# Which heads share a logits group in the sparse attention of a two-layer streaming encoder

## The reference, cut to what matters

```python
score = einsum('bqhs,bqh->bqs', relu(dots), wi)           # indexer, 8 heads of 64
top_val, top_idx = lax.top_k(score, k_top)                # 128 keys, 144 for the sample
qg = q.reshape(B, QB, N_KV_HEADS, KV_GROUP, HEAD_DIM)     # 8 heads = 2 KV heads x 4, each 64 wide
logits = einsum('bqngd,bqknd->bqngk', qg, k_sel) * HEAD_DIM ** -0.5
p = softmax(where(valid, logits, -inf))
o = einsum('bqngk,bqknd->bqngd', p, v_sel)
mix = concat([o, y_conv]); x = x + gt_a * (mix @ w_out)
```

## Time and profile before

| | |
|---|---|
| median of 3 runs | 1521.48 us (1521.14 to 1523.52) |
| the profiled execution | 1521.48 us |
| its span, first to last instruction | 1519.7 us |
| outside the span | 1.8 us |
| mean granted TensorE clock | 0.879 of 2.4 GHz |
| attention groups, layer 0 | about 333 to 436 us |
| attention groups, layer 1 | about 1078 to 1181 us |

### The profile page before, as it was taken

One profiled execution on the slowest core, in us unless ns is written; L12 is line 12 of the kernel. 1 busy time (PEld: TensorE's weight loads), 2 busy tenths in 40 slices (PEclk: granted clock), 3 DMA queues, 4 the chain that ended last, 5 costly groups with the idle time before them and its releaser, 6 DMA issues. The chain is left out here.

```text
span 1519.7 us, 14104 instructions
## 1 busy us (share of the span) xinstructions
PE 1218.0 (80%) x5211; PEld 726.5 (48%) x5211; DVE 752.3 (50%) x1541; ACT 336.3 (22%) x756; POOL 480.3 (32%) x292
## 2 busy tenths in 40 slices
PE   4699888945899878999708997896377995999980
PEld 0354525332445466777505544362245454777760
DVE  1109999787625521111151299998783353211114
ACT  2110231233431111111131003302535111111112
POOL 0005999443620120000020079995156011000002
PEclk9899999965999879999958998598758997999995
DMA  9961385340860579999581003011003016699975
GB/s 359 350 231 56 121 287 188 112 174 1 281 240 28 181 256 331 369 364 365 189 304 29 8 28 118 0 63 55 9 15 63 0 58 229 219 366 362 367 260 187
DMA packets 139300, 274.45 MB, mean 181 GB/s; under 512 B 16308, under 2 KB 98588, under 8 KB 132830
## 3 DMA queue, kind: packets, MB, share of 16 engines
q1 hardware_dynamic: 110272, 199.31, 38.2%
q10 hardware_dynamic: 22398, 50.63, 9.9%
q0 software_dynamic: 6560, 23.60, 4.3%
HBM read 237.89 MB, written 52.40 MB: 191 GB/s over the span
## 5 line engine op out<-in xcount | busy, mean ns | idle before, releaser
L409 PE MATMUL ps<-W,arena 128*128 128x256 f32 (+1 forms) x1280 | 348.4, 428 | 10.0 <-DMA W<-in_w_gate 4.6
L409 PEld LDWEIGHTS ps<-W,arena 128*128 128x128 f32 x1280 | 242.6, 193 | 85.6 <-issue 55.3
L419 PE MATMUL ps<-C,arena 128*128 128x128 f32 (+3 forms) x851 | 129.4, 301 | 113.1 <-DVE arena L1311 25.4
L409 PE MATMUL ps<-W,hT 128*128 128x512 f32 (+5 forms) x640 | 193.5, 463 | 1.6 <-DVE gt L1164 1.6
L419 PEld LDWEIGHTS ps<-C,arena 128*128 128x128 f32 (+3 forms) x851 | 107.8, 161 | 147.7 <-issue 52.6
L1238 DVE SCALAR_TENSOR_TENSOR arena<-arena,taps 128x606 f32<-128x606 f32 x180 | 158.9, 955 | 0.2
L1608 POOL TENSOR_TENSOR arena<-arena 128x512 f32<-128x512 f32 x8 | 89.6, 11202 | 208.0 <-ACT arena L898 208.0
L1666 POOL DMA_INDIRECT arena<-y_d,sid x20 | 20.2, 1009 | 404.4 <-DMA y_d<-arena 200.9
L409 PEld LDWEIGHTS ps<-W,hT 128*128 128x128 f32 (+1 forms) x640 | 103.5, 183 | 91.8 <-issue 82.4
L648 PE MATMUL ps<-W,hT 128*128 128x512 f32 (+1 forms) x320 | 143.3, 601 | 1.0 <-issue 1.0
L409 PE MATMUL ps<-hT,W 128*128 128x64 f32 (+1 forms) x512 | 140.5, 437 | 3.6 <-ACT hT L869 3.6
(11 more groups left out here) (217 smaller groups left out, 1167.5 us busy)
## 6 DMA issues: line engine op xcount, KB each, us to landing
W<-in_w_ada SPq DMA_DIRECT2D x48, 1024.0 KB, 6.5
W<-in_w_gate SPq DMA_DIRECT2D x32, 1024.0 KB, 10.6
W<-in_w_up SPq DMA_DIRECT2D x32, 1024.0 KB, 12.9
W<-in_w_down SPq DMA_DIRECT2D x32, 1024.0 KB, 7.8
arena<-x_d SPq DMA_DIRECT2D x33, 512.0 KB, 11.2
y_d<-arena ACTq DMA_DIRECT2D x33, 512.0 KB, 7.2
W<-in_w_in SPq DMA_DIRECT2D x16, 1024.0 KB, 14.6
W<-in_w_out SPq DMA_DIRECT2D x8, 1024.0 KB, 6.5
```

Source lines behind the costliest of these rows:

```text
L409: ins = T.matmul(out, l, r, start=n == 0, stop=n == len(pairs) - 1, skip_group_check=True)
L419: count(T.transpose(o, i, ident[0:m, 0:m]), done if n == len(outs_ins) - 1 else None)
```

## The change

Which four heads make a group is changed. Before, group (t, g) takes heads from both KV heads: jobs j = 0 to 3 are i = 2g, 2g, 2g + 1, 2g + 1, in the lower, upper, lower, upper half of the rows. After, group (t, g) takes the four heads of KV head g: all four jobs are in the same half, lower for g = 0 and upper for g = 1. The bank of a job and the waits are the same by job number.

PV follows: a group has one KV head, so one value matrix serves two heads in one product with twice the columns. There are half as many PV matmuls, each over 2m columns instead of m (m is 128, or 64 in the sample tile). `outputs` writes to `hT` chunks 2g, 2g + 1 instead of g, g + 2.

```diff
                 def logits(n):
-                    t, half = GROUPS[n]
+                    t, g = GROUPS[n]
                     a, b = keys_of(t)
-                    for j in range(4):
-                        job, i = 4 * n + j, 2 * half + j // 2
-                        hp = slice(64 * (j % 2), 64 * (j % 2) + 64)
+                    hp = slice(64 * g, 64 * g + 64)
+                    for i in range(4):
+                        job = 4 * n + i
                         if job >= 3:
                             pe.wait_ge(L["ttr"], job - 1 if 2 <= n <= 4 else job - 2)
                         q = qT[hp, i, tokens(t)]
...
-                    for q in range(2):
-                        for c, kn in chunks_of(t):
-                            v = (...)[:, 64 * q:64 * q + 64]
-                            heads = pT[0:kn, c, 0:4 * m].rearrange("p (a g t) -> p a g t", a=2, g=2)
-                            for a in range(2):
-                                ins = T.matmul(ps[6 + n % 2][64 * a:64 * a + 64, q * m:(q + 1) * m], v, heads[:, a, q, :],
-                                               start=c == 0, stop=c == last, skip_group_check=True)
+                    for c, kn in chunks_of(t):
+                        v = (...)[:, g * 64:g * 64 + 64]
+                        heads = pT[0:kn, c, 0:4 * m].rearrange("p (j a t) -> p j a t", j=2, a=2)
+                        for a in range(2):
+                            ins = T.matmul(ps[6 + n % 2][64 * a:64 * a + 64, 0:2 * m], v, heads[:, :, a, :],
+                                           start=c == 0, stop=c == last, skip_group_check=True)
...
-                    S.copy(hT[:, g:g + 3:2, t * P:t * P + m],
+                    S.copy(hT[:, 2 * g:2 * g + 2, t * P:t * P + m],
```

More of the change, by code:

```diff
@@ L608, in _ @@
                     pe.wait_ge(L["pta"], PT0[n] + len(chunks_of(t)))
-                    for q in range(2):
-                        for c, kn in chunks_of(t):
-                            v = (vrow[0:kn, c, :] if t < 4 else cv[:, c, :] if c < 4 else vrow[0:kn, 4, :])[:, 64 * q:64 * q + 64]
-                            heads = pT[0:kn, c, 0:4 * m].rearrange("p (a g t) -> p a g t", a=2, g=2)
-                            for a in range(2):
-                                ins = T.matmul(ps[6 + n % 2][64 * a:64 * a + 64, q * m:(q + 1) * m], v, heads[:, a, q, :],
-                                               start=c == 0, stop=c == last, skip_group_check=True)
+                    for c, kn in chunks_of(t):
+                        v = (vrow[0:kn, c, :] if t < 4 else cv[:, c, :] if c < 4 else vrow[0:kn, 4, :])[:, g * 64:g * 64 + 64]
+                        heads = pT[0:kn, c, 0:4 * m].rearrange("p (j a t) -> p j a t", j=2, a=2)
+                        for a in range(2):
+                            ins = T.matmul(ps[6 + n % 2][64 * a:64 * a + 64, 0:2 * m], v, heads[:, :, a, :],
+                                           start=c == 0, stop=c == last, skip_group_check=True)
                     ins.then_inc(L["pv"], 1)
```

## The result

The changed kernel takes 1539.6 us in the median (1535.7 to 1542.5) beside 1522.0 for the kernel before. The ratio is 1.0115 with a 95% interval of 1.0097 to 1.0133, so it is about 17.6 us slower. The forecast was 1530 with a range up to 1537: the sign was right, the size half of what came. The profiled execution took 1542.4 us (span 1540.4).

The account below looks back on a forecast made before the run. Attention was taken as a relay of engines, with logits groups on the path. 1521.5 us plus 8.7 for serial logits (4.3 in layer 0, 4.4 in layer 1) minus 0.1 for PV gave 1530.1, range 1525 to 1537.

Parts of the forecast that it names:

- the mechanism and its fixed price: Logits: jobs in opposite row halves overlapped, now run one after the other; 4.3 us in layer 0, 4.4 in layer 1.
- the forecast with clocks as before: Main case: TensorE's granted clock stays as it was, 1527 to 1533 us; 58 in 100.
- the 0 for groups 5 and 6 of layer 0: Logits of these two groups in layer 0: the serial order was claimed to cost 0 in each.
- the clock goes the wrong way: Rival, layer 1: 1.2 GHz lasts longer, group 2 +2.5 us or group 7 +3; 1532.5 or both 1535.5; 25 in 100.
- TensorE finishes three jobs before VectorE arrives: Group 5 of layer 0: the fourth job is alone anyway, so serial order costs 0.
- queues on GpSimd: Group 6 of layer 0: +0.2 at 2.4 GHz, but its normalising product waits behind group 5's, so 0.
- group 4 of layer 1: Logits: the same stall on VectorE as in layer 0, hidden since group 5 starts from GpSimd; 0.
- group 6 of layer 1: Logits over 384 keys at 1.2 GHz: serial 5.48 us against 4.06, +1.4.
- exposed loads: Rival: weight loads into the working row half can't be hidden, 12.8 us more, 1543; 3 in 100.
- nothing behind takes the delay in: After attention: no DMA wait absorbs the delay, so the rest shifts; output projections start at about 441 and 1190 us.
- Its own price: PV: paid by column, so half the matmuls at twice the columns gives -0.1 us; bounds -4.6 to +0.9.

Follow-up runs that it names:

- e0: The kernel before, unchanged, run again for a second profile and the scatter of its times; ratio 0.9999 (0.998 to 1.0017).
- e5: The changed kernel with PV cut back into narrow matmuls of one head each, a repeat on another chip; ratio 1.0090 (1.0063 to 1.0116).
- e2: The changed kernel with PV cut back into narrow matmuls of one head each; ratio 1.0056 (1.0033 to 1.0078).
- e9: The changed kernel with seven unused matmuls per layer in groups 3 and 4, where TensorE waits; ratio 1.0071 (1.0056 to 1.0086).
- e4: The changed kernel, unchanged, run again for a second profile; ratio 1.0117 (1.0093 to 1.0142).
- The twins: The changed kernel, each logits job of groups 2 to 9 followed by an unused equal product in the other row half; ratios 1.0019 and 1.0015.
- e6: The kernel before with a fourth PSUM bank for the logits of groups 4 to 9 of layer 1; ratio 0.9994 (0.9977 to 1.0011).
- e3: The changed kernel with an unused equal product in the other row half after each logits job of groups 2 to 9; ratio 1.0019 (1.0000 to 1.0038).
- e10: The changed kernel with the unused products in the other row half, a repeat; ratio 1.0015 (0.9999 to 1.0032).
- e7: The kernel before with seven unused matmuls per layer in groups 3 and 4, where TensorE waits; 1518.5 us, ratio 0.9971 (0.9957 to 0.9984).

## Why the prediction was wrong

**Right: the mechanism and its fixed price.** The halves overlapped and now follow each other; what the forecast worked out from passes came true to a few tenths wherever the clock was the same. That is group 2, 3 and 4 of layer 0, group 3 and 5 of layer 1. TensorE's time of group 6 at 1.2 GHz (5.49 against 5.48) and of group 7 at 2.4 (2.84 against 2.82) did too. At the clock that these groups had, serial order makes 3.85 us in layer 0, 1.18 + 0.89 + 1.34 + 1.43 in layer 1, and 0.25 in each group 7: 9.2 us against 8.7 forecast.

**Wrong: "the forecast with clocks as before", and with it the 0 for groups 5 and 6 of layer 0.** This is the step that failed; the premise had 58 in 100. Against it stand 2.71 and 4.55 us in groups 5 and 6 of layer 0, about 0.35 in group 7 there, and 2.47 in group 2 of layer 1: 10.1 us. The last was named, and priced at 0.3 + 2.5, in the rival "the clock goes the wrong way". Of its 2.47, the clock by itself is 0.70: so much longer is the same group in e0, which ran it at 1.2 GHz with overlapped jobs. The other 1.77 is serial order at that clock, as the 1.78 of layer 0. The rival looked at layer 1 only. In layer 0 the forecast had "TensorE finishes three jobs before VectorE arrives" and "queues on GpSimd": both hold about at 2.4 GHz. With serial logits, group 5 lost 0.52 us in e5, where 2.4 GHz was granted from 388.0 us on. Group 6 lost nothing in e2 (-0.3) and e9 (0.0), where it was granted from 400.3 and 402.2 us on; its eight serial passes took 2.84 us in both, where the changed kernel has 5.49. At 1.2 GHz, TensorE runs serial logits, modulation product and PV in 5.73 + 3.64 + 1.78 us without a gap, and is the bound itself. e0 shows that even the kernel before is at the edge there, since these two groups took 2.7 us more in its profile with nothing changed.

**Wrong: group 4 of layer 1, 0 forecast, 0.89 measured.** That GpSimd starts group 5 didn't hide it. ScalarE's exponentials of group 4 came later, the transposes of group 3 waited for ScalarE, and group 5's logits stand behind them on TensorE:

```profile
1144.76 1.46 PE L419 MATMUL ps<-C,arena 64*128 64x64 f32 x9 [1.37 <-ACT arena L1022]
```

**Half right: group 6 of layer 1.** TensorE did take 1.43 us longer, but only 0.33 to 0.75 arrived there, counted from the first profile. Ahead of it ScalarE's copy (L1005 before) came 1.16 us earlier after the exponentials: before it stood behind DMA issues for 2.85 us, after for 1.69:

```profile
1159.00 0.27 ACT L1004 COPY hT<-ps 128x128 f32<-128x128 f32 x1 [1.69 <-issue]
```

That is within the scatter and not shown to be the change's doing: the same wait is 1.51 us in e0, with nothing changed, and 2.11 in e4. In e0 the clock rose within the logits of group 6 (at 1146.7 us) and was at 1.2 GHz again from 1153.5 to 1156.9, where those of group 7 began. Counted from it, group 6 loses 2.41 us and group 7 gains 1.33. So the share of either is open; the two together lose 1.1 to 1.5 us, beside the 1.7 that serial order makes. The sum is 9.2 + 10.1 - 0.4 = 18.9 us, against 11.7 + 7.5 in the profiles (the 0.3 that is missing is group 1 of layer 1, which is as late in e0) and 17.6 in the comparison.

**Right: no exposed loads.** Serial passes take their columns (5.49 us for eight of 384, each with its own weight load), so the rival fell. The rule of the Trainium skill ("TensorE: Matmul & The Clock Gate", Part 3: Packing small matmuls) that a load overlaps only where the row group differs is not borne out here. **Right: nothing behind takes the delay in.** The output projections start at 451.4 and about 1201 us, later than the forecast's 441 and 1190 by what attention took more and where the layer began. From the first attention to the second 652.9 us pass after the change, and 655.6 and 651.1 in the two profiles of before.

**PV.** Its own price was right (0.1 us). A further cost of the wide form while the clock is low is likely, from none to 9 us, and not settled.

**The clock's cause, as far as shown.** The twins leave the order of the real jobs as it is, and the wait that they bring forward ended no idle time of TensorE in the attentions of their profiles. What they add is work in the other half of the array, and the clock follows. Fill in idle time lifts it as well, so whether it is the idle half or the amount of work that counts is not separated. The range should have followed: a change that can lower the clock needs a price for every stretch at 2.4 GHz that lies beside it, not for the one next to the known slow stretch.

## What to carry to other kernels

In these traces, products that use half of the rows are free in pairs: issue jobs of opposite halves next to each other, and don't group heads so that all of a group share a half. When a change makes TensorE's work sparser, price every neighbouring stretch at both clock levels, and see which engine is the bound in each. In a relay of four engines, what a slower step costs depends on which engine is the bound at that group, and what a faster one gains can go to the next wait (e6), so the two directions need separate estimates. And take two profiles of each kernel before you explain a single group: here they differ by up to 2.3 us in one group with nothing changed.

## What the runs showed that was not expected

- TensorE was busy without a gap from 393.4 to 403.7 us at 1.2 GHz, with half of its rows at work in 5.3 us of it.
- Twice the logits work made the changed kernel 14 to 15 us faster (e3, e10), and unused matmuls made the kernel before 4.1 us faster (e7), apart from its two executions of 1980 and 2542 us.
- The same kernel has 105.7 or 112.6 us at 1.2 GHz in its attentions, and attentions of 179.7 or 181.8 us.
